# Column-wise x for the first projection of an attention and convolution trunk

## What is computed

```python
def rms_norm(x, g):
    y = x * lax.rsqrt(jnp.mean(x * x, axis=-1, keepdims=True) + RMS_EPS)
    return y * g

hn = rms_norm(x, pre_norm_g[0])
proj = hn @ w_in                      # 256 x 2048 times 2048 x 8192
q, k, v, z = jnp.split(proj, 4, axis=-1)
# rotary q and k, causal attention in 16 heads, gate with silu(z), output projection,
# norm, residual; then the second layer: projection, gated unit, convolution over 31 rows
# (weights conv_w_dw), layer norm with gain and bias, gate, output projection, norm, residual
```

## Time and profile before

| | |
|---|---|
| time, median of 3 runs | 840.38 us (840.01 to 841.74) |
| span of the profiled execution, first to last instruction | 838.3 us |
| TensorE busy | 828.1 us, 99% |
| VectorE, ScalarE, POOL busy | 713.9, 423.9, 341.8 us |
| read from memory | 159.04 MB, 192 GB/s over the span |

### The profile page before, as it was taken

How to read it: one execution, slowest core, us unless ns; L and a number is a source line. 1 busy time by engine, 2 the same in 40 slices (tenths; PEclk the granted TensorE clock), 3 DMA queues, 4 the chain that set the end, 5 groups by cost and what they waited for, 6 DMA issues and landing times.

```text
span 838.3 us, 10938 instructions
## 1 busy us (share of the span) xinstructions
PE 828.1 (99%) x3807; PEld 686.0 (82%) x3807; DVE 713.9 (85%) x1234; ACT 423.9 (51%) x584; POOL 341.8 (41%) x171
## 2 busy tenths in 40 slices
PE   9999999999999999999999999999999999999996
PEld 6888888888888888888888788888888888888884
DVE  5588799988999799979857649999999999898655
ACT  6744534464444645454446574544454554574541
POOL 0342005500440004400000298888888878893000
PEclk9999999999999999999999999999999999999998
DMA  9956556656567555747555485555555545567522
GB/s 318 317 177 203 172 159 192 194 163 196 155 194 210 185 157 162 233 155 251 180 187 191 146 299 195 180 182 199 199 169 187 198 154 199 200 226 245 189 94 100
DMA packets 97657, 161.62 MB, mean 193 GB/s; under 512 B 3316, under 2 KB 38484, under 8 KB 97108
## 3 DMA queue, kind: packets, MB, share of 16 engines
q1 hardware_dynamic: 97572, 161.13, 59.0%
q10 hardware_dynamic: 48, 0.02, 0.0%
HBM read 159.04 MB, written 2.10 MB: 192 GB/s over the span
## 4 chain that ended last, share of the span: by engine, by line
PE 97%; issue 1%; DMA 0%; ACT 0%; DVE 0%; SPq 0%; DVEq 0%; POOLq 0%; POOL 0%; ACTq 0%
PE acc L447 29%; PE acc L448 29%; PE acc L449 29%; PE X L457 1%; PE acc L432 1%; PE acc L434 1%; PE acc L433 1%; PE X L448 1%; PE X L447 1%; PE X L449 1%; PE acc L513 1%; PE acc L528 1%; DMA raw<-in_w_in 0%; PE X L573 0%; PE X L584 0%
## 5 line engine op out<-in xcount | busy, mean ns | idle before, releaser
L791 ACT ACTIVATE w_hi<-raw 128x1024 fp32r<-128x1024 f32 x282 | 298.5, 1060 | 339.2 <-PE acc L449 326.5
L447 PE MATMUL acc<-w_hi,xT_hi 128*128 128x512 f32 x864 | 338.8, 392 | 0.0
L449 PE MATMUL acc<-w_hi,xT_lo 128*128 128x512 f32 x864 | 336.6, 390 | 0.0
L448 PE MATMUL acc<-w_lo,xT_hi 128*128 128x512 f32 x864 | 336.4, 389 | 0.0
L1075 DVE TENSOR_TENSOR w_lo<-raw,w_hi 128x1024 fp32r<-128x1024 f32 x180 | 242.2, 1362 | 69.4 <-ACT w_hi L791 67.0
L1563 POOL TENSOR_TENSOR w_lo<-raw,w_hi 128x1024 fp32r<-128x1024 f32 x102 | 248.5, 2444 | 45.1 <-ACT w_hi L791 44.6
L449 PEld LDWEIGHTS acc<-w_hi,xT_lo 128*128 128x128 f32 x864 | 162.2, 188 | 33.9
L447 PEld LDWEIGHTS acc<-w_hi,xT_hi 128*128 128x128 f32 x864 | 162.3, 188 | 33.3 <-DVE xT_lo L1094 0.2
L448 PEld LDWEIGHTS acc<-w_lo,xT_hi 128*128 128x128 f32 x864 | 162.3, 188 | 32.8
L1365 DVE SCALAR_TENSOR_TENSOR X<-u_pad,taps,X 128x256 f32<-128x256 f32 x464 | 183.6, 477 | 3.5 <-ACT X L1004 3.5
L1526 POOL TENSOR_TENSOR small<-small 128x1 f32<-128x1 f32 (+1 forms) x7 | 4.3, 617 | 220.8 <-DVE small L1292 122.9
(11 more groups left out here) (159 smaller groups left out, 793.2 us busy)
## 6 DMA issues: line engine op xcount, KB each, us to landing
raw<-in_w_in SPq DMA_DIRECT2D x78, 1024.0 KB, 5.3
raw<-in_w_in SPq DMA_DIRECT2D x66, 512.0 KB, 4.4
raw<-in_w_out SPq DMA_DIRECT2D x32, 1024.0 KB, 5.1
gpost<-in_post_g SPq DMA_DIRECT2D x2, 1024.0 KB, 5.8
brow<-in_b_in SPq DMA_DIRECT2D x1, 2048.0 KB, 10.2
xrow<-in_x SPq DMA_DIRECT2D x4, 256.0 KB, 5.2
raw<-in_w_in SPq DMA_DIRECT2D x4, 256.0 KB, 4.6
xrow<-in_x SPq DMA_DIRECT2D x2, 512.0 KB, 9.3
```

Source lines behind the costliest of these rows:

```text
L447: nc.tensor.matmul(a, hi[:, k, rows], w_hi[:, slot, i], start=(k == 0), stop=False)
L448: nc.tensor.matmul(a, hi[:, k, rows], w_lo[:, slot, i], start=False, stop=False)
L449: last = nc.tensor.matmul(a, lo[:, k, rows], w_hi[:, slot, i], start=False, stop=(k == KT - 1))
L791: nc.scalar.activation(w_hi[:, slot], raw[:, u % LOADS, 2 * half:2 * half + 2], ACT.Copy).then_inc(hi_ready[slot], 1)
```

## The change

- The host passes x a second time, by columns (`x_cols`: 128 partitions, 16 tiles, 256 rows), and all vectors and the taps with one channel to a partition (`vectors`, `tap_cols`), so that they land as they are used. The transposes of the vectors and their copies go.
- In the first layer the high and low parts of x are made from the SBUF copy of the columns, `x_col`, by `column_high` and `column_low`, with the arithmetic of before. The transposes of x in the first block go; those of the second layer stay.
- `x_col` is loaded in five chunks (1, 1, 2, 4 and 8 tiles; 128 KB a tile). ScalarE starts the first three and the vectors, SP the other two among its weight loads. SP starts with the weights.
- The row-wise x, now only for the squares and the residual, is loaded in two halves by columns after loads 0 to 3 and ahead of load 4.
- The squares move on ScalarE: three after pairs 4, 5 and 6, five after pair 7; 1 to 4 wait for the first half of x, 5 to 8 for the second.
- The identity is loaded behind the mask, the taps behind it. TensorE runs 8 matmuls on the empty tile at the start, in one go.

```diff
+X_CHUNKS = ((0, 1), (1, 2), (2, 4), (4, 8), (8, KT))
...
-SQUARES_AFTER = (1, 2, 3, 5)
+SQUARES_AFTER = (4, 5, 6)
...
+        x_col = at("x_col", B, [P, KT, SEQ])
...
-            def x_load(first, last):
-                c = slice(first * SEQ, (last + 1) * SEQ)
-                sp.dma_start(xrow[:, :, c], xv[:, :, c]).then_inc(x_in[x_chunk(first)], 16)
+            def x_load(i):
+
+                c = slice(i * D // 2, (i + 1) * D // 2)
+                sp.dma_start(xrow[:, :, c], xv[:, :, c]).then_inc(x_in[i], 16)
 
             def w_load(n, first, last, done):
 
                 k = 2 * SL_K * n
                 sp.dma_start(raw[:, n, first:last + 1], wv[:, k + first:k + last + 1, 0:NCOL]).then_inc(done, 16)
 
-            sp.dma_start(ident[:], identity).then_inc(ident_in, 16)
-            x_load(0, 0)
+            def col_load(i):
+
+                a, b = X_CHUNKS[i]
+                sp.dma_start(x_col[:, a:b], x_cols[:, a:b]).then_inc(col_in[i], 16)
+
             w_load(0, 0, 0, tile_in[0])
             w_load(0, 1, 1, tile_in[1])
-            x_load(1, 1)
             w_load(0, 2, 2, tile_in[2])
             w_load(0, 3, 3, raw_ready[0])
-            x_load(2, 2)
+            col_load(3)
             w_load(1, 0, 1, half_in)
-            x_load(3, 3)
             w_load(1, 2, 3, raw_ready[1])
-            x_load(4, 5)
+            col_load(4)
             load(S_QKVZ, 0, 32, 2, w_in0[0], 0)
-            x_load(6, 7)
             load(S_QKVZ, 0, 32, 3, w_in0[0], 0)
+            x_load(0)
+            x_load(1)
             load(S_QKVZ, 0, 32, 4, w_in0[0], D)
 
-            for v, rows, src in ((V_BA, 2 * KT, b_in), (V_BDW, KT, b_dw), (V_LNG, KT, ln_g), (V_LNB, KT, ln_b)):
-                sp.dma_start(vec_rows[v - NPRE:v - NPRE + rows, :], src.rearrange("l (t c) -> (l t) c", c=P)
-                             ).then_inc(vec_in, 16)
             sp.dma_start(cos_t[:], rope_cos).then_inc(rope_in, 16)
             sp.dma_start(sin_t[:], rope_sin).then_inc(rope_in, 16)
             sp.dma_start(mask[:], causal).then_inc(rope_in, 16)
-            sp.dma_start(dw_rows[:], w_dw[0].rearrange("k (t c) -> (k t) c", c=P)
-                         .rearrange("(q r) c -> r q c", r=DW_ROWS)).then_inc(dw_in, 16)
+            sp.dma_start(ident[:], identity).then_inc(ident_in, 16)
+            sp.dma_start(taps[:], tap_cols).then_inc(taps_in, 16)
...
             def first_block():
 
-                tile_products(0)
-                input_T(0, 1)
-                tile_products(1)
-                tile_products(2)
-                input_T(0, 2)
-                tile_products(3)
-                input_T(0, 3)
+                for t in range(2 * FINE):
+                    tile_products(t)
                 for h in range(FINE, SLICES):
                     if h < STAGED:
                         staged_products(h)
                     else:
                         pe.wait_ge(xlo_ready, h + 1)
                         slice_products(S_QKVZ, 0, 32, h, xT_hi, xT_lo)
-                    if h + 2 < SLICES:
-                        input_T(0, h + 2)
 
             def keep_clock(n):
...
-            keep_clock(4)
-            pe.wait_ge(ident_in, 16)
-            pe.wait_ge(pre_in, 16)
-            nc.tensor.transpose(X[3][:, 0:NPRE], pre_rows[:], ident[0:NPRE, 0:NPRE]).then_inc(vec_T, 1)
-            keep_clock(3)
-            input_T(0, 0)
-            keep_clock(2)
+            keep_clock(8)
             first_block()
...
-                    if s == 9 and first:
-                        pe.wait_ge(vec_in, 16 * 4)
-                        nc.tensor.transpose(X[1][:, 0:NVEC], vec_rows[:], ident[0:NVEC, 0:NVEC])
-                        pe.wait_ge(dw_in, 16)
-                        for q in range(4):
-                            last = nc.tensor.transpose(X[0][:, q * DW_ROWS:(q + 1) * DW_ROWS], dw_rows[:, q, :],
-                                                       ident[0:DW_ROWS, 0:DW_ROWS])
-                        last.then_inc(vec_T, 1)
                     if s == SCORES_AT:
-                        if first:
-                            pe.wait_ge(vec_ready, 2)
-                        else:
+                        if not first:
...
+            def column_high(h):
+
+                act.wait_ge(col_in[col_chunk(2 * h)], 16)
+                for t in (2 * h, 2 * h + 1):
+                    last = nc.scalar.activation(xT_hi[:, t], x_col[:, t], ACT.Copy,
+                                                scale=vec[:, V_PRE0 + t:V_PRE0 + t + 1])
                 last.then_inc(xhi_ready, 1)
...
-            act.dma_start(pre_rows[:], pre_g.rearrange("l (t c) -> (l t) c", c=P)).then_inc(pre_in, 16)
-
-
-            act.wait_ge(vec_T, 1)
-            nc.scalar.activation(vec[:, 0:NPRE], X[3][:, 0:NPRE], ACT.Copy).then_inc(vec_ready, 1)
-            act.wait_ge(vec_ready, 1)
+            def col_load(i):
+
+                a, b = X_CHUNKS[i]
+                act.dma_start(x_col[:, a:b], x_cols[:, a:b]).then_inc(col_in[i], 16)
+
+            col_load(0)
+            act.dma_start(vec[:], vectors).then_inc(vec_in, 16)
+            col_load(1)
+            col_load(2)
+            act.wait_ge(vec_in, 16)
...
             def tile_high(t):
 
                 h, c = t // 2, t % 2
                 if t:
-                    ready, n = of_tile(t, tile_T, xT_done, h + 1)
-                    act.wait_ge(ready, n)
-                    nc.scalar.activation(xT_hi[:, t], X[t][:, 0:SEQ], ACT.Copy,
-                                         scale=vec[:, V_PRE0 + t:V_PRE0 + t + 1]
-                                         ).then_inc(xhi_ready if c else tile_xhi, 1)
+                    act.wait_ge(col_in[col_chunk(t)], 16)
+                    nc.scalar.activation(xT_hi[:, t], x_col[:, t], ACT.Copy, scale=vec[:, V_PRE0 + t:V_PRE0 + t + 1]
...
-                    input_high(0, h, V_PRE0)
+                    column_high(h)
                 for s in SPLIT_AFTER[h]:
                     high(S_QKVZ, 0, 32, s)
                 if h in SQUARES_AFTER:
                     n = SQUARES_AFTER.index(h)
-                    wait_columns(n // 2)
+                    act.wait_ge(x_in[n // 4], 16)
                     input_squares(junk0[:], n // 2, n % 2, n)
             for n in range(len(SQUARES_AFTER), SLICES):
-                wait_columns(n // 2)
+                act.wait_ge(x_in[n // 4], 16)
                 input_squares(junk0[:], n // 2, n % 2, n)
 
...
-                    if s == 12 and first:
-                        act.wait_ge(vec_T, 2)
-                        nc.scalar.activation(vec[:, NPRE:NPRE + NVEC], X[1][:, 0:NVEC], ACT.Copy)
-                        nc.scalar.activation(taps[:], X[0][:, 0:TAPS * KT], ACT.Copy).then_inc(vec_ready, 1)
...
+            def column_low(h):
+
+                dve.wait_ge(xhi_ready, h + 1)
+                for t in (2 * h, 2 * h + 1):
+                    last = nc.vector.scalar_tensor_tensor(
+                        out=xT_lo[:, t], in0=x_col[:, t], scalar=vec[:, V_PRE0 + t:V_PRE0 + t + 1],
+                        in1=xT_hi[:, t].bitcast(f32), op0=ALU.mult, op1=ALU.subtract)
                 last.then_inc(xlo_ready, 1)
...
                 if t == 0:
-                    dve.wait_ge(vec_ready, 1)
-                    dve.wait_ge(tile_T, 1)
-                    nc.vector.tensor_scalar(xT_hi[:, 0], X[0][:, 0:SEQ], vec[:, V_PRE0:V_PRE0 + 1], None, ALU.mult
-                                            ).then_inc(tile_xhi, 1)
-                ready, n = of_tile(t, tile_xhi, xhi_ready, h + 1)
+                    dve.wait_ge(vec_in, 16)
+                    dve.wait_ge(col_in[0], 16)
+                    nc.vector.tensor_scalar(xT_hi[:, 0], x_col[:, 0], vec[:, V_PRE0:V_PRE0 + 1], None, ALU.mult
+                                            ).then_inc(tile_xhi[0], 1)
+                ready, n = of_tile_x(t, h + 1)
                 dve.wait_ge(ready, n)
                 nc.vector.scalar_tensor_tensor(
-                    out=xT_lo[:, t], in0=X[t][:, 0:SEQ], scalar=vec[:, V_PRE0 + t:V_PRE0 + t + 1],
+                    out=xT_lo[:, t], in0=x_col[:, t], scalar=vec[:, V_PRE0 + t:V_PRE0 + t + 1],
...
+    by_column = lambda a: np.asarray(a).reshape(-1, KT, P).transpose(2, 1, 0)
...
+        x=x, x_cols=by_column(x[0]), tap_cols=by_column(conv_w_dw[0]).transpose(0, 2, 1).reshape(P, TAPS * KT),
+        vectors=np.concatenate([by_column(v)[:, :, i] for v, i in (
+            (pre_norm_g, 0), (pre_norm_g, 1), (conv_b_in.reshape(2, D), 0), (conv_b_in.reshape(2, D), 1),
+            (conv_b_dw, 0), (conv_ln_g, 0), (conv_ln_b, 0))], axis=1),
```

More of the change, by code:

```diff
@@ L84, with build @@
 TURN_P, VALUES_AT, GATE_ROWS_AT, TURN_U, SPLIT_U = 2, 4, 7, 8, 13
-DW_ROWS = TAPS * KT // 4
-def build(nc, x, pre_g, post_g, w_in0, w_out0, w_in1, b_in, w_dw, b_dw, ln_g, ln_b, w_out1, b_out,
+def build(nc, x, x_cols, vectors, tap_cols, post_g, w_in0, w_out0, w_in1, b_in, w_out1, b_out,
           rope_cos, rope_sin, identity, causal, out):
@@ L196, in build @@
```

(62 more changed lines are left out.)

37 lines of the change are left out of this document (16 added, 21 removed).

## The result

| | before | after |
|---|---|---|
| time, median of 12 runs each, side by side | 840.77 us | 842.92 us (842.35 to 843.32) |
| ratio after to before, 95% interval | | 1.0021 (1.0013 to 1.0029) |
| span of the profiled execution | 838.3 us | 840.5 us |

A forecast was written before the change was run, and what follows sets the result against it. TensorE's matmul queue bounds the kernel, its early start set by arriving bytes: slice 8 2.5 us later, less 0.50 for vector transposes, is 2.0 slower; added to 840.38 (2.1 over the span), 842.4 us, range 839.6 to 844.3.

The forecast's parts named there:

- the case's own range: Whole kernel: 840.7 to 843.4 us, from the fast and slow ends of the early transfers' landing.
- What is removed: TensorE, first block: seven pairs of x transposes, 3.2 us, and vector and tap transposes, 0.50 us, the latter gain kept.
- The start: Ahead of the first product: ScalarE's table load falls behind the weight tile's landing; first product at 6.0 us, not 4.6.
- The bytes: Early transfers: first half of row-wise x lands at 23.2 us, load 4 at 28.4 (26.7 to 29.4).
- The quick end of the range: Early transfers: first half of row-wise x at 21.6 us, with 390 GB/s from the start and 437 for wide pieces.
- Who waits: ScalarE and TensorE, slices 4 to 8: idle 2.7 and 3.0 us ahead of slices 4 and 5; slice 8 2.5 later.
- Hidden: Mean of squares behind pair 7, up to slice 10: covered with 1.8 us to spare; beyond it each us costs one.
- the fourth rival: Mean of squares, q_row, then rope on POOL: covers of 1.8 us too thin, about 2 us more, 844.4; chance 0.05.
- The first (rates add): Early transfers: two queues' rates add, x at 21.7 us, so not slower: 840.9, or 839.2 with fast pieces; chance 0.17.
- the rule on queues in the prediction: Early transfers: queues of different engines share the same 16 DMA engines; a second saves only time of issue.
- The third (all comes through): First block: whole saving kept, slice 8 4.4 us earlier plus 0.50, 835.5; needs x by 17.0; chance 0.06.
- The second (the clock): TensorE, slices 5 to 7: clock falls behind gaps of 2.7 and 3.0 us; 843.8 taken, up to 845; chance 0.12.

The follow-up runs named there:

- the vectors alone: Kernel before with only vectors and taps loaded one channel to a partition, their transposes and copies gone, x as it was: 842.95 us, ratio 1.0026.
- early table load: One-element ACTIVATE put ahead of ScalarE's waits: on the kernel after 843.00 us; on the kernel before with only the vectors and taps changed 840.12 us.
- the first: Kernel after with all eight squares behind pair 7, transfers unchanged: 843.56 us, ratio 1.0041.
- second: Kernel after with both halves of the row-wise x loaded behind load 4, squares left in place: 846.32 us, ratio 1.0066.
- fourth kernel: Kernel after with both halves of the row-wise x behind load 4 and all squares behind pair 7: 839.87 us, ratio 0.9991.
- the filled gaps: Kernel after with empty matmuls put before slices 4 (ten), 5 (ten) and 7 (two): 843.47 us, ratio 1.0030.
- the third: Kernel after with only the second half of the row-wise x loaded behind load 4: 842.96 us, ratio 1.0023.
- one queue: Kernel after with ScalarE starting no transfer; SyncE issues columns and vectors just ahead of their weight tiles: 844.44 us, ratio 1.0041.
- the split columns: Kernel after with x behind load 4, squares behind pair 7, q turned two slices later, last column chunk split around load 2: 838.33 us, ratio 0.9971.

## Why the prediction was right, and where it was not

The forecast was +2.0 us and 842.4; +2.15 and 842.92 were measured, inside the case's own range. Step by step:

- **What is removed.** Right in kind. That TensorE's busy time fell by just the 3.2 and 0.5 put down is in part luck: 0.7 of the 3.7 us lies ahead of the first product (3.60 us busy there, 4.30 before), where nothing waited for it. The 0.50 of the vectors was kept, as the sum at slice 8 shows; with the vectors alone, early table load or not, it can't be told from no change.
- **The start.** The table load went behind the landing, as forecast, and the first product was at 6.35, 0.35 later than the 6.0 put down. The load cost little here, since the vectors landed only at 5.2, as VectorE's first instruction shows, and the early load won 0.2. Mis-sized was the landing of the first columns: the prediction allowed 0.5 us for waits in slices 0 to 3, and tiles 1 and 2 waited 0.72 and 1.45 on ScalarE. Slice 3 ended at some 18.9 (17.95 and four steps of 0.23), not at 17.4. It cost nothing at the end, because slice 4 waited for load 2 in any case: its gap was 1.3 us by the profile where 2.7 was put down.
- **The bytes.** Row-wise x 23.1 us (put down: 23.2), load 2 17.9 (17.7), load 4 28.4 (28.4). The quick end of the range was not reached: the rate before 8 us rose from 277 to 296 GB/s, worth 0.1 MB or 0.3 us, and from 8 to 22 us from 373 and 390 to 393 and 400, worth another 0.5; 437 was nowhere reached. How much of that is due to the pieces of 4 and 8 KB no run separates. That 23.2, a choice between 21.6 and 24.0, came within 0.1 is partly luck.
- **Who waits.** Slice 4 at 20.34 (20.1), slice 5 at 25.70 (25.8), slice 7 at 31.95 (32.0), slice 8 at 34.96 (34.7). The gap ahead of slice 5 was put at 3.0 and is 2.5 by the dense pace. A pair from SBUF takes 0.89 on ScalarE, with 0.80 to the next start, and 0.88 on VectorE; the sum had 0.84, 0.72 and 0.88. That both limits, ScalarE's wait and load 4, had to go before the time fell is shown by the first, second and fourth kernel; the prediction had them in one chain.
- **Hidden.** The cover of 1.8 us held in after: TensorE has no idle time to speak of behind slice 8. It was as thin as the fourth rival had it: with slice 8 3.4 us earlier, 1 us was lost there, shown by moving the turning of q.
- **The rivals.** The first (rates add) fell: from 2 to 8 us, with both queues at work, 296 GB/s flowed, less than the 390 of one queue later, and x landed at 23.1. What it saw right is that the queue helps, but by issue time, 1.5 us. It is this rival, not the third, that the rule on queues in the prediction stands against. The third (all comes through) fell with the landing: it needed x by 17.0. The second (the clock) is not in the profiled execution of after, but it is in several experiments. Of the twelve runs of after, the five with a mean granted clock of 0.994 or 0.995 took 843.0 to 843.3 us, the two with 0.998 842.35 and 842.36, and the five with 0.996 842.5 to 843.3. That is about the 0.7 us worked out for some 3 us at the lower level, in five executions of twelve. But runs of before spread by as much, 840.0 to 842.2 at clocks of 0.996 to 0.998, and the mean doesn't say where the clock fell: with the filled gaps it was 0.995 with no fall in the gaps, and with the early table load 0.996 with a fall that cost nothing. A load 4 that lands late in some executions would give the same spread. So it is a fit and not shown.

The time itself, 842.92, lies 0.5 over the 842.4 put down. Of that 0.4 is the start of the sum: before took 840.77 over twelve runs, not the 840.38 of the first three. The rest is the 0.15 between +2.0 and +2.15.

## What to carry to other kernels

Taking work off the bound engine wins only what the next late thing allows: here that was the arrival of the bytes, and reading x twice put 2.1 MB more ahead of load 4 (8.45 MB, 6.37 before), and it landed 4.4 us later. Count the bytes ahead of each first use, in order of issue, and put last what is needed last; and on an engine that works in order, put no instruction whose data come late ahead of others that could run. Where two waits end close together, take both away before judging either.

## What the runs showed of the hardware

- TensorE's clock fell to its lower level behind a gap of 2.84 us in the kernel with the squares last (granted 0.58 from 32 to 36 us, steps of 0.43 us instead of 0.23), behind 5.11 in the second, behind 2.38 us as the profile gives it in the third, 2.36 with one queue, and 1.84 with the early table load. It did not fall behind 2.38 in the profile of after, nor behind 1.92 in the fourth kernel: the length of the gap alone doesn't decide. The Trainium skill (TensorE: Matmul & The Clock Gate, section "Why this matters for your kernels") advises against gaps of over about 3 us; all of these falls but that behind 5.11 came below it, so the prediction's reading of the rule, that the clock would stay, does not hold here.
- The column of the granted clock is no guide at the start: with the split columns the first products step by 0.43 us while it says 1.00 (the first row's two start at 8.12, and the next two follow at 8.97).

```profile
8.12 1.05 PE L520 MATMUL acc<-w_lo,xT_hi 128*128 128x512 f32 x2
...
6.00:10.00 4.00, 3.73 (x10) 1.00 0.93 352
```

- Where a table load stands depends on the waits ahead of its ACTIVATE: at 1.19 us, before any data, with a single wait (before); with two at 4.29 in after and 5.58 with the vectors alone, in both behind the landing of the weight tile.
- Small transfers on a second queue were slow beside a full first one: the third column chunk, 256 KB, took 7.2 us from issue to landing, where it took 5.8 on SP's queue alone. But it stood at another place in the order there, so not all of that need be the queue.

```profile
x_col<-in_x_cols ACTq DMA_DIRECT2D x1, 256.0 KB, 7.2
...
x_col<-in_x_cols SPq DMA_DIRECT2D x1, 256.0 KB, 5.8
```
